# A decoder step on one core: the input's norm inside the projection, a reload in 24 pieces, and pages as the stationary operand

## The reference

```python
h = rmsnorm(x, ln_pre_mix); parts = split(h @ w_in)          # 1024 -> 3352 columns
ret = retention(rq, rk, rv)                                  # 8 heads of 64, state carried
# native sparse attention, 8 heads in 2 groups, three branches:
o_cmp = softmax(q . kc) @ vc        # keys and values compressed by blocks of 64
o_sel = attention over the 16 chosen blocks of the selected cache (pages by a table)
o_win = attention over the last 512 tokens
mix = concat(silu(g) * groupnorm(ret), gated sum of the three) @ w_o
h = x + rmsnorm(mix)
y = h + rmsnorm(square(relu(rmsnorm(h) @ w_up)) @ w_down)    # 1024 -> 4096 -> 1024
```

## Time and profile before

| | |
|---|---|
| Time, median of 3 runs | 1870.74 us (1869.11 to 1871.97) |
| The profiled execution | 1874.87 us, span 1872.8 us |
| TensorE busy | 1722.4 us, 92% of the span |
| VectorE, ScalarE, GpSimd busy | 840.7, 633.4, 136.3 us |
| Mean granted clock of TensorE | 0.964 |
| DMA | 147.93 MB, mean 79 GB/s |

### The profile page before, as it was taken

How to read it: one execution, slowest core, us unless ns; L and a number is a source line. 1 busy time by engine, 2 the same in 40 slices (tenths; PEclk the granted TensorE clock), 3 DMA queues, 4 the chain that set the end, 5 groups by cost and what they waited for, 6 DMA issues and landing times. The chain is left out here.

```text
span 1872.8 us, 29665 instructions
## 1 busy us (share of the span) xinstructions
PE 1722.4 (92%) x11649; PEld 1514.6 (81%) x11649; DVE 840.7 (45%) x1644; ACT 633.4 (34%) x1305; POOL 136.3 (7%) x236
## 2 busy tenths in 40 slices
PE   3999999993999669999988999999999999999897
PEld 2989988993864645555548889999999999999897
DVE  4566442131116366667756675322332233223366
ACT  5222322210010146676645554301320132023343
POOL 1000000014234300000000110000000000000000
PEclk8999999997999789999988999999999999999999
DMA  7111111125876500000007633211111111111444
GB/s 273 46 47 47 34 47 41 46 63 142 200 196 177 158 16 1 1 1 1 1 1 206 177 118 102 64 47 54 48 46 46 46 46 45 48 54 46 158 126 145
DMA packets 215436, 147.93 MB, mean 79 GB/s; under 512 B 13213, under 2 KB 205090, under 8 KB 214978
## 3 DMA queue, kind: packets, MB, share of 16 engines
q1 hardware_dynamic: 179970, 98.33, 18.8%
q0 software_dynamic: 12288, 37.21, 6.4%
q10 hardware_dynamic: 23040, 10.50, 2.2%
HBM read 133.71 MB, written 16.47 MB: 80 GB/s over the span
## 5 line engine op out<-in xcount | busy, mean ns | idle before, releaser
L1943 PE MATMUL psum<-act_hi,whi 128*128 128x344 f32 x960 | 310.5, 323 | 8.5 <-DVE wlo L2062 5.5
L1943 PE MATMUL psum<-act_lo,whi 128*128 128x344 f32 x960 | 307.7, 321 | 0.0
L1943 PE MATMUL psum<-act_hi,wlo 128*128 128x344 f32 x960 | 307.6, 320 | 0.0
L2062 DVE TENSOR_TENSOR wlo<-wraw,whi 128x1024 fp32r<-128x1024 f32 x111 | 136.0, 1226 | 265.9 <-ACT whi L1959 265.7
L1943 PE MATMUL psum<-hidden_hi,whi 128*128 128x344 f32 x768 | 247.2, 322 | 8.8 <-issue 8.8
L1943 PE MATMUL psum<-hidden_hi,wlo 128*128 128x344 f32 x768 | 245.8, 320 | 0.0
L1943 PE MATMUL psum<-hidden_lo,whi 128*128 128x344 f32 x768 | 245.7, 320 | 0.0
L1959 ACT ACTIVATE whi<-wraw 128x1024 fp32r<-128x1024 f32 x111 | 117.4, 1057 | 350.8 <-PE psum L1943 326.2
L231 PE MATMUL psum<-act_hi,whi 128*128 128x344 f32 x648 | 213.9, 330 | 9.0 <-DVE wlo L263 9.0
L231 PE MATMUL psum<-act_hi,wlo 128*128 128x344 f32 x648 | 207.4, 320 | 0.0
L231 PE MATMUL psum<-act_lo,whi 128*128 128x344 f32 x648 | 207.4, 320 | 0.0
(11 more groups left out here) (366 smaller groups left out, 2513.3 us busy)
## 6 DMA issues: line engine op xcount, KB each, us to landing
wraw<-in_w_down SPq DMA_DIRECT2D x48, 512.0 KB, 3.7
wraw<-in_w_up SPq DMA_DIRECT2D x40, 512.0 KB, 4.1
wraw<-in_w_in SPq DMA_DIRECT2D x27, 512.0 KB, 3.8
wraw<-in_w_o SPq DMA_DIRECT2D x23, 512.0 KB, 3.9
h_features<-mixed_then_h POOLq DMA_DIRECT2D x24, 172.0 KB, 2.7
h_again<-h_features POOLq DMA_DIRECT2D x3, 1376.0 KB, 11.4
x_rows<-in_x_prompt SPq DMA_DIRECT2D x4, 1024.0 KB, 9.5
dec_pages<-in_cache_sel_k SPq DMA_DIRECT2D x64, 64.0 KB, 3.1
```

The lines of the kernel that those rows point to most:

```text
L1943: last = pe.matmul(ps[:, u % 3, 0:TN], wt[:, kt, :], xt[:, kt, cols], start=(kt == 0 and i == 0), stop=(kt == KT - 1 and i == 2))
L2062: dve.tensor_tensor(m.wlo[p % 2][:], wraw[raw_slot[p]][:], m.whi[p % 2][:].bitcast(F32), ALU.subtract).then_inc(lo_ready, 1)
```

## The change

Three edits, in one step.

1. `stage_prepare` is gone as a stage, and with it its barrier. A class `Prepare` holds its instructions, and the programs of `stage_project` call them. The decoded rows are scaled first; their eight transposes go into one bank, with one `hi` and one `lo` for all. The first weight tile is loaded behind half of x. The first half of the tokens is normed, the first chunk multiplied, then the second half normed; units go through four banks (3 to 6) instead of six. POOL's window copies wait for the constants instead of x.
2. `h_again` is loaded in 24 pieces of one feature tile and one chunk, the n-th when n units of the last 24 are done.
3. In the V products the page is the stationary operand and 8 columns of `pT` (the sequence's own heads) are the moving one; everything is added into one 128x64 tile with features on the partitions, the common part first. The chain behind is replaced by four copies on VectorE and four on ScalarE.

```diff
-def stage_prepare(nc, m, ps, io):
...
+class Prepare:
...
+    def pool_part(self, pool):
...
+        pool.wait_ge(self.const_loaded, 16)
+        for old, new in (("cache_win_k", "win_k_sample"), ("cache_win_v", "win_v_sample")):
...
+    def act_start(self, act):
+        act.wait_ge(self.xs_loaded, 16)
+        act.activation(self.junk[0:DEC, :], self.xs[:], ACT.Square, accum_out=self.sums[0:DEC, NB:NB + 1]).then_inc(self.squares, 1)
+        self.act_squares(act, 0, 4)
+        self.act_root(act, 2)
+        self.act_root(act, 0)
+        act.wait_ge(self.ln_turned, 1)
+        act.activation(self.m.lnT[:], self.ps[:, 7, 0:36], ACT.Copy).then_inc(self.ln_ready, 1)
+        self.act_squares(act, 4, 6)
...
+    def dve_scale(self, dve, h):
+        self.dve_rstd(dve, h)
+        for t in range(4 * h, 4 * h + 4):
+            dve.tensor_scalar(self.x[:, t, :], self.x[:, t, :], self.rstd[:, t:t + 1], None, ALU.mult).then_inc(self.scaled, 1)
...
+    def pe_turn(self, pe, h):
+        pe.wait_ge(self.scaled, 4 * h + 5)
+        for kt in range(KT):
+            u = 8 * h + kt
+            if u >= 4:
+                pe.wait_ge(self.lo_done, u - 3)
             for i in range(4):
...
+    def pe_wait_chunk(self, pe, t):
+        pe.wait_ge(self.lo_done, 8 if t == 0 else 16)
+        if t == 2:
+            pe.wait_ge(self.xs_lo, 1)
@@ stage_project, sync @@
+            inp.load_x(sp, 0)
+            inp.load_ident(sp)
+            inp.load_x(sp, 1)
             for n, c in enumerate(COLUMNS):
                 w.load(sp, n, n % 2, raw_src[:, :, c:c + P])
+                if n == 0:
+                    inp.load_x(sp, 2)
+                    inp.load_x(sp, 3)
+                    inp.load_const(sp)
@@ tensor @@
+            inp.pe_start(pe)
+            inp.pe_turn_decoded(pe)
+            inp.pe_turn(pe, 0)
             for turn, slot in slots:
+                if turn == 0 and slot < 3:
+                    inp.pe_wait_chunk(pe, slot)
                 w.multiply_chunk(pe, 4 * turn + slot // 3, slot % 3)
+                if turn == 0 and slot == 0:
+                    inp.pe_turn(pe, 1)
@@ scalar @@
+            inp.act_start(act)
             w.round_hi(act, 0, 0, 0)
+            inp.act_decoded(act)
+            inp.act_hi(act, 0)
+            inp.act_squares(act, 6, 8)
+            inp.act_root(act, 1)
+            inp.act_hi(act, 1)
@@ vector @@
             w.start_loads(dve)
+            inp.dve_scale_decoded(dve)
+            inp.dve_scale(dve, 0)
+            inp.dve_norm_decoded(dve)
             w.reduce_lo(dve, 0, 0, 0)
+            inp.dve_lo_decoded(dve)
+            inp.dve_lo(dve, 0)
+            inp.dve_scale(dve, 1)
+            inp.dve_lo(dve, 1)
+            inp.dve_casts(dve)
@@ gpsimd @@
+            inp.pool_part(pool)
             load_state(0)
@@ stage_cache, tensor @@
-            common = ps[0:ROWS, 4, 0:P]
+            features = ps[:, 4, 0:ROWS]
             for c in range(4):
-                pe.matmul(common, pT[:, 20 + c, :], m.vcs[:, c, :], start=(c == 0), stop=False)
+                pe.matmul(features, m.vcs[:, c, :], pT[:, 20 + c, :], start=(c == 0), stop=False, skip_group_check=True)
...
             for b in range(DEC):
+                rows = slice(b * NH, (b + 1) * NH)
                 wait_loaded(pe, v_loaded, b % 4, b // 4 + 1)
                 for i in range(20):
-                    e = i % 2
-                    last = pe.matmul(ps[e * ROWS:(e + 1) * ROWS, 5 + b // 4, (b % 4) * P:(b % 4 + 1) * P], pT[:, i, :],
-                                     pages[b % 4][:, i, :], start=(i < 2), stop=(i >= 18))
+                    last = pe.matmul(features[:, rows], pages[b % 4][:, i, :], pT[:, i, rows], start=False, stop=(i == 19),
+                                     skip_group_check=True)
                 last.then_inc(v_used, 1)
-            pe.wait_ge(out_dve, 5)
-            pe.transpose(ps[:, 3, 0:ROWS], o_row[:], m.c("ident")[0:ROWS, 0:ROWS]).then_inc(out_turned, 1)
@@ scalar @@
-            for i in range(2):
-                act.wait_ge(v_used, 4 * i + 4)
-                act.activation(o_odd[:, 4 * i:4 * i + 4, :], ps[ROWS:P, 5 + i, :].rearrange("p (b f) -> p b f", f=P), ACT.Copy).then_inc(odd_out, 1)
+            act.wait_ge(v_used, DEC)
+            for h in range(R, NH):
+                act.activation(m.mixT[(h % 2) * HD:(h % 2 + 1) * HD, 4 + h // 2, SEQ:TOK], ps[HD:P, 4, h:ROWS:NH], ACT.Copy).then_inc(placed, 1)
@@ vector @@
-            out = Steps(out_dve)
...
+            dve.wait_ge(v_used, DEC)
+            for h in range(R):
+                dve.tensor_copy(m.mixT[(h % 2) * HD:(h % 2 + 1) * HD, 4 + h // 2, SEQ:TOK], ps[0:HD, 4, h:ROWS:NH]).then_inc(placed, 1)
@@ stage_tail, gpsimd @@
-            pool.wait_ge(unit_done, y_start)
             for c in range(3):
                 pool.wait_ge(h_stored[c], 16 * KT)
-                pool.dma_start(m.h_again[:, :, chunk(c)], h_rows[:, :, chunk(c)]).then_inc(h_loaded[c], 16)
+                for kt in range(KT):
+                    pool.wait_ge(unit_done, y_start + KT * c + kt)
+                    pool.dma_start(m.h_again[:, kt, chunk(c)], h_rows[:, kt, chunk(c)]).then_inc(h_loaded[c], 16)
@@ vector @@
-                        dve.wait_ge(h_loaded[c], 16)
+                        dve.wait_ge(h_loaded[c], 16 * KT)
```

More of the change, by code:

```diff
@@ L302, in evacuated, with __init__ @@
         return n * 3 + (3 + t + 1)
-def stage_prepare(nc, m, ps, io):
-    with Stage(nc, "prep") as ctx:
+class Prepare:
+    def __init__(self, ctx, m, ps, io):
         s = ctx.semaphore
[L309 to L330, removed]
-            for i in range(4):
[L332 to L400, removed]
-        @block.tensor
-        def _(pe):
-            pe.wait_ge(ident_loaded, 16)
-            pe.wait_ge(ln_loaded, 80)
-            pe.transpose(ps[:, 7, 0:36], lnrows[:], m.c("ident")[0:36, 0:36]).then_inc(ln_turned, 1)
-            for u, (kt, h) in enumerate(units):
-                if u >= 6:
-                    pe.wait_ge(lo_done, u - 5)
-                if h < 2:
-                    pe.wait_ge(scaled, 4 * h + 4)
-                    for i in range(4):
-                        last = pe.transpose(ps[:, u % 6, i * P:(i + 1) * P],
-                                            x[:, 4 * h + i, kt * P:(kt + 1) * P], m.c("ident"))
-                else:
-                    pe.wait_ge(scaled, NB + 1)
-                    last = pe.transpose(ps[:, u % 6, 0:DEC], xs[:, kt * P:(kt + 1) * P],
-                                        m.c("ident")[0:DEC, 0:DEC])
-                last.then_inc(turned, 1)
@@ new lines, in act_squares, with act_root @@
+    def act_squares(self, act, first, end):
+        for t in range(first, end):
+            if t % 2 == 0:
+                act.wait_ge(self.x_loaded[t // 2], 16)
+            act.wait_ge(self.squares, t + 1)
+            act.activation(self.junk[:], self.x[:, t, :], ACT.Square, accum_out=self.sums[:, t:t + 1]).then_inc(self.squares, 1)
+    def act_root(self, act, h):
+        part = self.rstd[:, 4 * h:4 * h + 4] if h < 2 else self.rstd[0:DEC, NB:NB + 1]
+        act.wait_ge(self.mean_ready, (2, 3, 1)[h])
+        act.activation(part, part, ACT.Sqrt).then_inc(self.root_ready, 1)
@@ new lines, in act_decoded, with dve_rstd @@
+    def act_decoded(self, act):
+        act.wait_ge(self.xs_normed, 1)
+        act.activation(self.m.hi[:, :, SEQ:TOK], self.xsT[:], ACT.Copy).then_inc(self.xs_hi, 1)
+    def dve_rstd(self, dve, h):
+        rows = slice(0, P if h < 2 else DEC)
+        part = slice(4 * h, 4 * h + 4) if h < 2 else slice(NB, NB + 1)
+        n = (2, 3, 1)[h]
+        dve.wait_ge(self.squares, (5, 9, 1)[h])
+        dve.tensor_scalar(self.rstd[rows, part], self.sums[rows, part], 1.0 / D_MODEL, EPS, ALU.mult, ALU.add).then_inc(self.mean_ready, 1)
+        dve.wait_ge(self.root_ready, n)
+        dve.reciprocal(self.rstd[rows, part], self.rstd[rows, part]).then_inc(self.rstd_ready, 1)
+        dve.wait_ge(self.rstd_ready, n)
@@ L422, in stage_project, with pe_turn_decoded @@
+    def pe_turn_decoded(self, pe):
+        pe.wait_ge(self.scaled, 1)
+        pe.wait_ge(self.ln_ready, 1)
+        for kt in range(KT):
+            last = pe.transpose(self.ps[:, 7, 64 + kt * DEC:64 + (kt + 1) * DEC], self.xs[:, kt * P:(kt + 1) * P], self.m.c("ident")[0:DEC, 0:DEC])
+        last.then_inc(self.xs_turned, 1)
+    def pe_wait_chunk(self, pe, t):
+        pe.wait_ge(self.lo_done, 8 if t == 0 else 16)
+        if t == 2:
+            pe.wait_ge(self.xs_lo, 1)
 def stage_project(nc, m, ps, io):
```

85 lines of the change are left out of this document (64 added, 21 removed).

## The result

The changed kernel takes 1880.25 us (median of five runs, 1879.3 to 1888.1) against 1871.97 us before (1869.11 to 1875.19): slower, by a ratio of 1.0059 with a 95% interval of 1.0041 to 1.0077, so by 8 to 14 us; the medians differ by 8.3. Its profiled execution took 1879.3 us, with a span of 1877.4 and a mean granted clock of 0.957.

What follows compares the result with a forecast made beforehand. TensorE, busy for 92% of the span, was taken as the bound, with time to gain only where it waits or works slowly. Start -10.4, reload -10.3 and V products +29.9 sum to +9.2 us: median 1880, range 1870 to 1891.

Steps and rivals of the forecast that it cites:

- Start, -10.4 us: Kernel start: with stage and barrier gone, chunk 1 begins at 38.5 instead of 48.9, saving 10.4 us.
- Reload, -10.3 us: Reload of h_again: 24 pieces remove the 8.8 us wait and 1.5 us from half clock, saving 10.3 us.
- V products, +29.9 us: Decode's V products: 320 passes at half clock, 0.205 us each, cost +35.8; the shorter chain gives -5.9.
- the 32 one-column passes: Row before the V products (613.99 to 615.97), taken as nearest to the new form, hence half clock.
- the short end: Behind the V products: four copies on each of two engines, 0.95 us, replace the old chain: -5.9.
- Sum, +9.2: Whole kernel: -10.4 - 10.3 + 29.9 = +9.2 us, so the median becomes 1880.
- The rival of the other side: V products: full clock rises within the first batch, so the sum is -21.8 and the time 1849; chance 0.18.
- that mostly load weights: V products: passes mostly loading weights seem not to hold the clock up, so half clock for all 160 products.
- the fall at 616.9: Before the V products: the clock fell after one-column passes and less than 1 us idling; evidence for half clock.
- the idle 1.6 us at 22.65: Kernel start: idle gap to 24.26 between transposes, said to cost nothing; set against the clock's fall at 616.9.
- the start's bound: Kernel start: largest gain claimed, -11.5 us without hand-overs; the smallest was -7.5.
- The ends of the range: Likeliest case: 1871 (0.18 us a pass) to 1891 (0.224 a pass, 3 us less of the gains).

Runs made afterwards that it cites:

- e3: The kernel before with the new start alone: 1860.93 us, ratio 0.9947 to the kernel before.
- e1: The changed kernel with the V products and the chain behind them as before; new start and 24 pieces stay: 1849.29 us, 0.9883 to the kernel before.
- e4: The kernel before with the reload in 24 pieces alone: 1860.91 us, ratio 0.9941 to the kernel before.
- e2: The kernel before with the V products' operand swap alone: 1901.40 us, ratio 1.0165 to the kernel before.
- e12: The changed kernel with 15 unread products of 512 columns ahead of the V products: 1881.62 us, ratio 1.0061 to the kernel before.
- e11: The changed kernel with 128 moving columns in the V products, 8 of them used: 1850.24 us, ratio 0.9893 to the kernel before.
- e6: The changed kernel with all 64 columns of the probabilities moving through each page: 1882.05 us, ratio 1.0059 to the kernel before.
- e10: The changed kernel with the V products as before (64 stationary columns, alternate halves, four buffers) but a shorter chain: 1843.88 us, 0.9860 to the kernel before.
- e7: The changed kernel with the sequence's own 8 columns stationary, the page moving, and a shorter chain: 1853.26 us, 0.9904 to the kernel before.
- e5: The changed kernel with an extra unread 512-column product ahead of every fifth V product, 32 in all: 1944.56 us, 1.0397 to the kernel before.

## Why the prediction was right

**Start, -10.4 us.** Measured alone: -10.4 (e3). Chunk 0 was to begin at 26.2 and began at 26.46; chunk 1 at 38.5, began at 37.81. In the profiled execution 1.5 us of it went to the clock's fall at 38.6, which the prediction didn't have and which e1's trace doesn't show. The 0.7 us that chunk 1 came early and this fall, which e3's trace has too, partly cancel, so the agreement to a tenth is partly luck.

**Reload, -10.3 us.** Measured alone: -10.5 (e4). No piece held up TensorE; y's first stores went out at 1854.97, behind the last piece, and cost nothing. The end at half clock, 1.3 us in the trace, was not foreseen.

**V products, +29.9 us.** Measured alone: +30.0 (e2); by its absence, 1880.25 - 1849.29 = +31.0 (e1; 30.4 when each is taken against the kernel before beside it). The clock was half, as taken from the 32 one-column passes. There was no wait for pages. The size is partly luck. A pass took 0.214 instead of 0.205, so the stretch 68.4 us instead of 65.6; the short end gave 6.0 instead of 5.9. In the traces the edit therefore costs 32.9 us from the first V product to the next stage (70.4 in e2 and 70.5 after, 37.5 before), 3 us more than the prediction and than the median of e2. Spells of half clock elsewhere differ by as much between traces; where the runs take the 3 us back is not shown.

**Sum, +9.2.** Medians: +8.3; the three edits alone, added: +9.1.

**The rival of the other side** (full clock, 1849) fell for the reason given, and its price was right: with the clock up the same passes start 0.112 apart (e12), and e11 ran in 1850.

**What was not right in the reasoning** is its wording that passes "that mostly load weights" don't hold the clock up. It rested on one row, the fall at 616.9. The row set against it, the idle 1.6 us at 22.65 that "cost nothing", is no contrast: the transposes ahead of that gap start 0.213 us apart and those behind it 0.109, so there was no full clock to lose. And loading is not the hindrance in itself, since e11's passes load the same weights and brought the clock up. What the rows bear out is this: passes that moved 8 or 64 columns through 128 columns of weights stayed at 0.50 (e2, e6), those of 8 did not bring it back (e12), passes that moved 128 columns each brought it up with 128, 64 and 8 columns of weights (e11, e10, e7), and wide products between narrow ones did not (e5). What in the chip decides that stays open.

Some side figures don't come out of the prediction's own terms; none enters its sum. Without hand-overs the start's bound is 38.2 - 48.9 = -10.7, not -11.5. The waits for pages in the old V stretch are 2.79 + 2.75 + 0.48 = 6.0 us, a fifth of it and not half. The ends of the range come out at 1872 and 1889 instead of 1871 and 1891, and the time measured lies between either pair.

The Trainium skill (TensorE: Matmul & The Clock Gate, "Why this matters for your kernels") advises keeping TensorE continuously busy to get to the higher clock. The traces disagree for this form: it was busy without a gap for 68.44 us at 0.50, and in e12 the clock fell while it was busy. Widening the 8 moving columns to 128 (e11) gained 30 us.

The Trainium skill's figure for a weight load (same page, "LDWEIGHTS (loading the stationary operand)", 107 ns for 128 columns) agrees with a pass of 0.111 at full clock and not with 0.214 at half. By it the prediction's own terms give an estimate of -22 us for the sum, not -20: 320 x 0.107 = 34.2 us from 630.4 on, -1.5 for the edit with its short end. For 64 columns the figure would be 53 ns (an estimate), and the 32 passes with one moving column agree at full clock, 1.98 / 32 = 0.06 us. For 8 columns it would be 7 ns; e7's passes took 0.108, and they move 128 columns, so there the load is not what sets the pass.

## What to carry to other kernels

Count what a product moves as well as what it loads: exchanging the operands turned 128 moving columns into 8, saved nothing on TensorE, and left its clock at half for the whole stretch. Before making a stretch of matmuls leaner, see whether it is TensorE that ends its waits; here it was the pages, and two buffers more gave 9 us. Large reloads go in pieces between the transfers that have a due time, and a norm can run beside the products that already have their input: each gave 10 us, and they added up.

## What was not expected of the hardware

- At one clock a pass took the same time with 8 and with 64 moving columns (68.44 and 68.53 us for 320), and at full clock nearly the same with 8 and with 128 columns of weights against 128 moving ones (0.108 and 0.111 us, e7 and e11). With one moving column and 64 columns of weights it took 0.06, with 8 moving and 128 of weights 0.112 (e12). So in these rows a pass goes with the larger of the two, columns loaded or columns moved.
- Passes of 64 columns of weights that go by turns into the two halves of the partitions took half as long: at full clock two start together every 0.109 us, so 0.055 each (e10). It is the halves that do this and not the 64 columns: in the trace of before, eight passes with 64 columns of weights and 128 moving ones that all go into one half start 0.213 us apart at clock 0.50, where the V products take 3.25 / 31 = 0.105.

```profile
627.82 1.97 PE L1144 MATMUL psum<-cmp_v_decoded,dec_pT 128*64 128x128 f32 x8 [0.62 <-ACT dec_p_newT L1218]
```

- The same attention, instruction for instruction, took 315.8 to 321.7 us in the traces, through spells of half clock that come at other places each time. A difference of 5 us between two single traces means nothing here; the medians of e1 to e4 add up within 1.2 us.
